# Row terms of the decay matrices as the bias of ScalarE's exponentials, in a two-block fp32 network on one core

## The reference, cut to what matters

```python
a_cs = jnp.cumsum(dtc * a, axis=2)
seg = a_cs[:, :, :, None] - a_cs[:, :, None, :]
lower = jnp.tril(jnp.ones((L, L), dtype=bool))[None, None, :, :, None, None]
decay = jnp.exp(jnp.where(lower, seg, -jnp.inf))
y_diag = jnp.einsum('bclsg,bclsgr,bcsgrp->bclgrp', cb, decay, xd)
```

```python
d_log = jnp.where(causal, b[..., :, None] - b[..., None, :] + ig[..., None, :], -jnp.inf)
m_t = jnp.maximum(inter_log, jnp.max(d_log, axis=-1))
scores = jnp.einsum('bhctd,bhcsd->bhcts', q, k) * jnp.exp(d_log - m_t[..., None])
```

## Time and profile before

| what | value |
|---|---|
| median of 3 runs | 1845.61 us (1844.77 to 1845.63) |
| the profiled execution's own time | 1845.08 us |
| its span | 1843.3 us |
| PE busy | 1828.3 us (99%) |
| DVE busy | 1266.7 us (69%) |
| ACT busy | 1055.9 us (57%) |
| POOL busy | 100.5 us (5%) |
| chain that ended last, by engine | PE 95%, ACT 3%, DVE 1% |

### The profile page before, as it was taken

One profiled execution on the slowest core, in us unless ns is written; L12 is line 12 of the kernel. 1 busy time (PEld: TensorE's weight loads), 2 busy tenths in 40 slices (PEclk: granted clock), 3 DMA queues, 4 the chain that ended last, 5 costly groups with the idle time before them and its releaser, 6 DMA issues.

```text
span 1843.3 us, 28625 instructions
## 1 busy us (share of the span) xinstructions
PE 1828.3 (99%) x11626; PEld 1628.1 (88%) x11626; DVE 1266.7 (69%) x1944; ACT 1055.9 (57%) x1557; POOL 100.5 (5%) x85
## 2 busy tenths in 40 slices
PE   9999999999999999999999999999999999999999
PEld 9998998789998999899789998988878888887887
DVE  6764797766665665588876665687667567875755
ACT  6444767565444444576755544475776456568642
POOL 0000110000000000020000000002001000210100
PEclk9999999999999999999999999999999999999999
DMA  8555542345555556553325555554445555534553
GB/s 292 193 191 182 188 151 100 106 137 189 192 193 186 190 195 194 180 179 112 126 92 172 191 193 189 173 184 147 139 137 182 194 163 182 171 126 137 172 192 116
DMA packets 86596, 310.09 MB, mean 168 GB/s; under 512 B 9648, under 2 KB 10288, under 8 KB 86464
## 3 DMA queue, kind: packets, MB, share of 16 engines
q1 hardware_dynamic: 85680, 306.35, 50.7%
q0 software_dynamic: 496, 1.65, 0.2%
q10 hardware_dynamic: 288, 0.25, 0.0%
HBM read 307.16 MB, written 1.05 MB: 167 GB/s over the span
## 4 chain that ended last, share of the span: by engine, by line
PE 95%; ACT 3%; DVE 1%; issue 0%; DMA 0%; POOL 0%; SPq 0%; DVEq 0%; ACTq 0%
PE bank L1162 92%; PE bank L1159 3%; ACT PA L1579 1%; DVE PA L2686 0%; ACT MP L1579 0%; ACT WH L1579 0%; ACT L1579 0%; DVE WL L2034 0%; DMA X<-in_x_dram 0%; ACT ET L1579 0%; DVE PC L2711 0%; DVE STATS L2384 0%; ACT BZ L1579 0%; DVE BO L2676 0%; DVE X L2120 0%
## 5 line engine op out<-in xcount | busy, mean ns | idle before, releaser
L2034 DVE TENSOR_TENSOR WL<-RAW,WH 128x1024 fp32r<-128x1024 f32 x585 | 704.6, 1213 | 405.0 <-ACT WH L1579 403.4
L1579 ACT ACTIVATE WH<-RAW 128x1024 fp32r<-128x1024 f32 (+2 forms) x587 | 610.1, 1050 | 497.0 <-PE bank L1162 494.2
L1162 PE MATMUL bank<-WH,FR 128*128 128x512 f32 x1264 | 318.4, 390 | 0.0
L1162 PEld LDWEIGHTS bank<-WH,FR 128*128 128x128 f32 x1264 | 233.7, 188 | 48.4 <-issue 0.8
L1162 PE MATMUL bank<-XTH,WH 128*128 128x256 f32 x1792 | 254.4, 279 | 0.6 <-ACT XTH L1579 0.6
L1162 PE MATMUL bank<-XTH,WL 128*128 128x256 f32 x1792 | 251.9, 278 | 0.0
L1162 PE MATMUL bank<-XTL,WH 128*128 128x256 f32 x1792 | 251.1, 277 | 0.0
L1162 PEld LDWEIGHTS bank<-XTH,WH 128*128 128x128 f32 x1792 | 226.9, 188 | 1.5 <-issue 0.8
L1162 PEld LDWEIGHTS bank<-XTH,WL 128*128 128x128 f32 x1792 | 226.7, 188 | 0.0
L1162 PEld LDWEIGHTS bank<-XTL,WH 128*128 128x128 f32 x1792 | 226.0, 188 | 0.0
L1162 PE MATMUL bank<-WL,FR 128*128 128x512 f32 x632 | 173.7, 389 | 0.0
(11 more groups left out here) (337 smaller groups left out, 1850.6 us busy)
## 6 DMA issues: line engine op xcount, KB each, us to landing
RAW<-in_WALL_dram SPq DMA_DIRECT2D x569, 512.0 KB, 3.3
RAW<-in_WALL_dram SPq DMA_DIRECT2D x8, 448.0 KB, 3.3
RAW<-in_WALL_dram SPq DMA_DIRECT2D x8, 256.0 KB, 2.6
X<-in_x_dram SPq DMA_DIRECT2D x4, 256.0 KB, 5.5
out_dram<-X SPq DMA_DIRECT2D x4, 256.0 KB, 2.0
ROWP<-in_ROWP_dram POOLq DMA_DIRECT2D x1, 672.0 KB, 11.0
CONSTS<-in_CST_dram POOLq DMA_DIRECT2D x1, 664.0 KB, 7.9
ROUNDED<-in_CSTR_dram POOLq DMA_DIRECT2D x1, 208.0 KB, 12.2
```

The costliest lines, as they stand in the source:

```text
L1162: return self.e.matmul(out, lhs, rhs, start=start, stop=stop, skip_group_check=True)
L1579: return self.e.activation(out, in_, func, **k)
L2034: self.e.tensor_tensor(lo, raw, hi.bitcast(F32), ALU.subtract).then_inc(*self.up("lo", j))
```

## The change

The row terms leave PE and become the bias operand of ACT's exponential. A bias is one number per partition, so a bank needs one instruction for each head and direction: four of 128 columns in place of one of 512 in `seg`, two (256 and 128 columns) in place of one of 384 in `mse`. The bias tiles are `BI` (in `SPT`), made from the logarithms of the step sizes less the cumulated sums that `ex` leaves in its bank, by a new DVE phase `ex`; and `BIH` (in `SP2`), copied by ACT from two more transposes in `chain` 7. The tile `LN` and its POOL memset go, `cum` loses its four products with `LN`, `DA` is made by four DVE instructions in place of eight, and the low part of `LBH` and of `LB` is made for 32 partitions in place of 64.

```diff
@@ PE.cum, PE.seg, PE.chain, PE.mse
-                self.mm(o, k.DA[:, t, d, :], (k.LE, k.GE)[d], t == 0 and d == 0, False)
-                m = self.mm(o, k.LN[:, t, d, :], k.EYE, False, True)
+                m = self.mm(ps[:, 256 * t + 128 * d:256 * t + 128 * d + 128], k.DA[:, t, d, :], (k.LE, k.GE)[d],
+                            t == 0 and d == 0, True)
...
-            self.mm(ps[:, :, x, :], k.TO[:, h0 + x:h0 + x + 1].to_broadcast([128, 128]),
-                    k.LBH[:, 256 * t:256 * t + 256].rearrange("p (d s) -> p d s", d=2), False, False)
-        for d in range(2):
-            m = self.mm(ps[:, d, :, :], k.LBH[:, 256 * t + 128 * d:256 * t + 128 * d + 128],
-                        k.FROM[:, h0:h0 + 2].unsqueeze(2).to_broadcast([128, 2, 128]), False, d == 1)
+            m = self.mm(ps[:, :, x, :], k.TO[:, h0 + x:h0 + x + 1].to_broadcast([128, 128]),
+                        k.LBH[:, 256 * t:256 * t + 256].rearrange("p (d s) -> p d s", d=2), False, x == 1)
...
+            for t in range(2):
+                m = self.tr(ps[:, 128 + 128 * t:256 + 128 * t], k.G2[:, 3, 128 * t:128 * t + 128])
...
-        self.mm(ps[:, 0:256], k.LB[:, 0:128], frm.to_broadcast([128, 256]), False, False)
-        self.mm(ps[:, 256:384], k.LB[:, 128:256], frm.to_broadcast([128, 128]), False, True).then_inc(*self.up("mse_pe", (i, h)))
@@ Scalar.seg, Scalar.mse
-        self.act(k.ET[:, n % 4, :], k.PS[k.bank["seg", i, n]][:, :], ACT.Exp).then_inc(*self.up("et_act", (i, n)))
+        g, t, q = n // 8, n // 4 % 2, n % 4
+        w.wait_ge(*self.at("ex_dve", i))
+        for d in range(2):
+            for x in range(2):
+                at, h = 256 * d + 128 * x, 8 * g + 2 * q + x
+                m = self.act(k.ET[:, n % 4, at:at + 128], k.PS[k.bank["seg", i, n]][:, at:at + 128], ACT.Exp,
+                             bias=k.BI[:, t, d, h:h + 1])
+        m.then_inc(*self.up("et_act", (i, n)))
...
-        self.act(k.E2[:, h % 3, :], k.PS[k.bank["mse", i, h]][:, 0:384], ACT.Exp).then_inc(*self.up("ms_act", (i, h)))
+        w.wait_ge(*self.at("em_act", i))
+        for t, c0, c1 in ((0, 0, 256), (1, 256, 384)):
+            m = self.act(k.E2[:, h % 3, c0:c1], k.PS[k.bank["mse", i, h]][:, c0:c1], ACT.Exp, bias=k.BIH[:, t, h:h + 1])
+        m.then_inc(*self.up("ms_act", (i, h)))
@@ Vector.ex
+        w.wait_ge(*self.at("ex_act", i))
+        w.wait_ge(*self.at("decay_act", (i, "ln")))
+        e.tensor_tensor(k.BI, k.BI, ps, ALU.subtract).then_inc(*self.up("ex_dve", i))
@@ WORK
-    "cum": "P198 A60 V140", "ex": "P281 A27",
+    "cum": "P90 A60 V70", "ex": "P170 A27 V20",
-    "seg": "P53 A61 V90",
+    "seg": "P56 A124 V90",
-    "mse": "P68 A40 V71",
+    "mse": "P42 A65 V71",
```

More of the change, by code:

```diff
@@ L757, in pair @@
             if p == 0:
-                for phase in (("chain", i, 6), ("hconv_silu", i, 0), ("hconv_silu", i, 1), ("evict", ("bv", i, 0))):
+                for phase in (("chain", i, 7), ("hconv_silu", i, 0), ("hconv_silu", i, 1), ("evict", ("bv", i, 0))):
                     yield phase
@@ L1742, in decay @@
             w.wait_ge(*self.at("decay_dve", (i, "ln")))
-            self.act(k.LN[:, :, :, 64:80], k.LN[:, :, :, 64:80], ACT.Ln)
-            self.act(k.LN[:, :, :, 96:112], k.LN[:, :, :, 96:112], ACT.Ln).then_inc(*self.up("decay_act", (i, "ln")))
+            self.act(k.BI, k.BI, ACT.Ln).then_inc(*self.up("decay_act", (i, "ln")))
     def lat_sq(self, i, t):
@@ L1900, in chain @@
             w.wait_ge(*self.at("chain_pe", (i, 7)))
-            self.act(k.EM[:, :, :], k.PS[k.bank["chain", i, 7]][:, 0:128].rearrange("p (t h) -> p t h", t=2)[:, :, 0:8],
-                     ACT.Exp, scale=-1.0).then_inc(*self.up("em_act", i))
+            ps = k.PS[k.bank["chain", i, 7]]
+            self.act(k.BIH, ps[:, 128:384].rearrange("p (t h) -> p t h", t=2)[:, :, 64:72], ACT.Copy)
+            self.act(k.EM[:, :, :], ps[:, 0:128].rearrange("p (t h) -> p t h", t=2)[:, :, 0:8], ACT.Exp, scale=-1.0).then_inc(
+                *self.up("em_act", i))
     def lam(self, i, x):
@@ L1995, in program @@
             "qk_sum": self.qk_sum, "qk_norm": self.qk_norm, "rope1": self.rope1, "qk_rope": self.qk_rope, "sc": self.sc,
-            "mo_a": self.mo_a, "mo_var": self.mo_var, "mo_y": self.mo_y, "cum": self.cum,
+            "mo_a": self.mo_a, "mo_var": self.mo_var, "mo_y": self.mo_y, "cum": self.cum, "ex": self.ex,
             "state_x": self.state_x, "fin": self.fin, "seg": self.seg, "skip": self.skip, "mid": self.mid, "fin_y": self.fin_y,
@@ L2277, in decay @@
             w.wait_ge(*self.at("pads_pool", i))
-            for at in (64, 96):
-                m = e.tensor_scalar(k.LN[:, :, :, at:at + 16], k.DT[:, :, :].rearrange("p t (d h) -> p t d h", d=2), 1e-18, None, ALU.max)
-            m.then_inc(*self.up("decay_dve", (i, "ln")))
+            e.tensor_scalar(k.BI, k.DT[:, :, :].rearrange("p t (d h) -> p t d h", d=2), 1e-18, None, ALU.max).then_inc(
+                *self.up("decay_dve", (i, "ln")))
             for d in range(2):
                 a = k.SPT[:, 5, 16 * d:16 * d + 16].unsqueeze(1).to_broadcast([128, 2, 16])
-                e.tensor_tensor(k.DA[:, :, d, 64:80], k.DT[:, :, 16 * d:16 * d + 16], a, ALU.mult).then_inc(*self.up("decay_dve"))
-            w.wait_ge(*self.now("decay_dve"))
-            for d in range(2):
-                for at, sgn in ((96, 1.0), (0, -1.0), (32, -1.0)):
-                    m = e.tensor_scalar(k.DA[:, :, d, at:at + 16], k.DA[:, :, d, 64:80], sgn, None, ALU.mult)
+                for at in (0, 32):
+                    m = e.scalar_tensor_tensor(k.DA[:, :, d, at:at + 16], k.DT[:, :, 16 * d:16 * d + 16], -1.0, a, ALU.mult, ALU.mult)
             m.then_inc(*self.up("decay_dve", (i, 3)))
@@ L2418, in cum, with ex @@
         w.wait_ge(*self.at("cum_act", i))
-        e.tensor_tensor(k.LBH[32:64, :], ps[32:64, :], k.LBH[32:64, :].bitcast(F32), ALU.subtract)
-        e.tensor_tensor(k.LBH[96:128, :], ps[96:128, :], k.LBH[96:128, :].bitcast(F32), ALU.subtract).then_inc(*self.up("cum_dve", i))
+        e.tensor_tensor(k.LBH[32:64, :], ps[32:64, :], k.LBH[32:64, :].bitcast(F32), ALU.subtract).then_inc(*self.up("cum_dve", i))
+    def ex(self, i):
+        k, w, e = self.k, self.w, self.e
+        ps = k.PS[k.bank["ex", i]][:, 0:128].rearrange("p (t d x) -> p t d x", t=2, d=2)[:, :, :, 0:16]
+        w.wait_ge(*self.at("ex_act", i))
+        w.wait_ge(*self.at("decay_act", (i, "ln")))
+        e.tensor_tensor(k.BI, k.BI, ps, ALU.subtract).then_inc(*self.up("ex_dve", i))
     def state_x(self, i, d):
@@ L2795, in mix_pads @@
         e.memset(k.PR[:, :, 257:258], 0.0)
-        e.memset(k.LN[:, :, :, :], 0.0)
         e.memset(k.DA[:, :, :, :], 0.0).then_inc(*self.up("pads_pool", i))
```

18 lines of the change are left out of this document (8 added, 10 removed), and 8 rows, old and new, of the table WORK.

## The result

| | before | changed |
|---|---|---|
| median | 1845.44 us (1844.77 to 1845.63, 4 runs) | 1855.76 us (1853.03 to 1858.18, 4 runs) |
| ratio to before | | 1.0056, 95% interval 1.0044 to 1.0069 |
| the profiled execution's own time | 1845.08 us | 1858.18 us |
| its span | 1843.3 us | 1856.3 us |
| mean granted TensorE clock | 1.000 | 0.996 |

The account below looks back on a forecast made before the run. PE, busy 99% of the span, was taken to bound the kernel. From 1845.1 us, mixers add 4.0, hybrid layers take off 1.4, and 0.5 is added for the median: 1848.2 us, range 1837 to 1857.

Parts of the forecast that it names:

- Products removed: On PE in mixers, hybrid layers and cum: 7.0 + 3.5 + 1.8 us removed, 0.9 added for transposes, net 11.4 us less.
- ACT's prices: On ACT: a four-piece segment bank takes 1.16 us, 0.57 more; the bias operand 0.09; an mLSTM bank grows by 0.25.
- Rival 2: In both segment stretches ACT becomes the bound, over 0.2% slower from 1.23 us a bank: 1853 to 1860 us, chance 0.22.
- The walk up to the flips: First mixer's segments, walked: waits of 0.2 to 2.1 us at cn_a, cn_b and several applies; stretch ends at 43.0.
- The 6.4 us of new waits: In a mixer's segment stretch: 2.9 us longer though PE's products are 3.5 us less, so 6.4 us of new waits.
- The mixer's term: Each mixer: segments 2.9 us longer, less 0.9 in cum, so 2.0 us more; 4.0 for two.
- Hybrid layers: Both hybrid layers together: 2.6 us kept from the products less 1.2 lost in the attention, 1.4 us faster.
- The mLSTM part: mLSTM banks of the hybrid layers: ACT's longer exponentials stay hidden behind a weight block, so 3.5 - 0.9 = 2.6 us are kept.
- the new order in the attention: Differential attention: head 3's exponentials stand behind the eviction of BO, between two table loads; 0.6 us a layer, 1.2 in all.
- the split behind head 3: Hybrid layers' attention: PE waits 1.9 us for a split (WH) behind head 3; some 1.3 us of waiting go in exchange.
- Rival 3: Shifted order changes waits of attention heads or the hybrid layers' last stretch by 3 to 5 us either way; chance 0.08.
- The full price of the removed products: On PE: all of the net 11.4 us less work counts on the path as long as PE has no new wait.

Follow-up runs that it names:

- seg_only: Kernel before with only the mixers' part of the change (seg, cum, ex, BI), in the old phase order: 1852.05 us, ratio 1.0029.
- mse_only: Kernel before with only the hybrid layers' part of the change (mse, chain 7, BIH, LB), in the old phase order: 1842.20 us, ratio 0.9981.
- fill: Changed kernel plus ten products of 512 columns on PE in each mixer, ahead of the block that waits for FR: 1852.63 us, ratio 1.0033.
- order_new: Kernel before, code unchanged, with the changed numbers in WORK and so the changed kernel's phase order: 1856.28 us, ratio 1.0058.
- no_from: Kernel before without the two row-term products of each segment bank, ACT and order unchanged: 1842.23 us, ratio 0.9983.
- pieces_bias: Kernel before with each segment exponential as four of 128 columns with a bias operand, all products kept, old order: 1855.78 us, ratio 1.0052.
- after_again: The changed kernel run and profiled again, unchanged: 1856.77 us, ratio 1.0059 to the kernel before.
- fix_ys: Changed kernel with the last fin_y of each mixer moved behind the two flips of the scaled rows: 1854.71 us, ratio 1.0050.
- code_old: Changed code with the old numbers in WORK for seg, mse, cum, ex and chain7, so the old phase order: 1848.64 us, ratio 1.0014.

## Why the prediction was right in range and wrong in size

- **Products removed: right.** `cum` gained 0.9 us a mixer (in `seg_only` the distance falls from 0.04 at `RBC,CONSTS` to -0.86 at `DA,CONSTS` behind it), eight mLSTM banks gained 1.8 us in `mse_only`. PE's records fell by 108: by the 112 of the prediction, and rose by 4, not 8, since a transpose is one record. The four transposes cost 0.4 us together, not 0.9.
- **ACT's prices: right.** A bank of four was put at 1.16 us and takes 1.14; the operand at 0.09 and takes 0.375 - 0.289 = 0.086; an mLSTM bank was to grow by 0.25 and takes 0.73 where it took 0.49. Rival 2's condition, a bank of 1.23 us or more, was not met. The estimate of 1.27 us from the Trainium skill ("ScalarE: Activation LUTs", "What ACT_TABLE_LOAD costs") was 0.13 too high, its 93 ns for the operand fits.
- **The walk up to the flips: right to the place, too high in most sizes.** In the first mixer it gave `cn_a` 0.55 more (0.76 was measured: 1.05 less the 0.29 of the earlier trace rows), `apply` 0 0.4 (0.25), the second `cn_b` 0.9 (0.61), the two later ones 1.1 and 0.25 (0.17 in all), `apply` 8 2.1 (1.42), `apply` 10 1.35 (1.11), and 0.2, 0.25 and 0.5 at `apply` 1, `apply` 3 and the flips (nothing). The rows in brackets are idle time; by the starts of the products `apply` 8 comes 1.58 us late and `apply` 10 1.27. It had the stretch end at 43.0 us; from the first `seg` at 344.80 to the end of the flips at 386.87 it is 42.1, but the block behind them starts at 389.40, after 44.6.
- **The 6.4 us of new waits: right in size by luck.** The walk's own list adds up to 7.6 us; the 6.4 of the sum are the difference of the two ends. Measured are 4.3 us of new idle time up to the flips, and 2.5 us behind them, for `FR`, which the walk didn't have.
- **The step that failed: the walk stopped at the flips.** "The two flips behind the last `apply` wait 0.5 for the scaled rows. The changed stretch ends at 43.0." They don't wait; but the block behind them needs `FR`, and on ACT the `YT` of the last `fin_y` stands ahead of it. With the rows of before it could have been walked: `YT` waits for two `XS` on DVE, which come after `apply` 15 and a split in DVE's list, and PE's 2.53 us for `FR` behind it are the largest single wait of the changed kernel. The walk looked for places where an exponential is late and stopped behind the last one; ACT is late beyond it.
- **A rival that was missing: the clock.** The sum took every wait at its own length. Behind these waits PE ran at 1.2 GHz for a while, 1.7 us of lost full-speed time in the first mixer of the profiled run and some 5 in the second (part of it while PE was idle anyway), and `fill` points to PE's idleness as what does it. The Trainium skill, "TensorE: Matmul & The Clock Gate", section "HAM oscillation — how this bites in real kernels", tells of a kernel in which PE waits for a DMA after each short piece of its work and starts the next piece at the slow clock. The waits there are longer than any here, so it was a warning against this change and no price for it; the traces agree with it in kind, by the 3.56 us of the block behind the 2.53 us of waiting. The earlier trace rows shows 1.00 for the kernel before, whose waits in that stretch are 0.3 us at most, which made the term easy to leave out.
- **The mixer's term** was thus 2.0 us and was 4.3 to 4.6 in most cases, up to 7.0 with two drops. With the clock up (`fill`, second mixer) it is 2.7.
- **The range held the time by luck.** Its upper part was there for a bank that costs ACT more than the 1.16 us taken. The bank costs 1.14, and what filled that part are the wait for `FR` and the clock.
- **Hybrid layers: sign right, terms smaller and larger.** The mLSTM part gave 3.3 us, not 2.6, and the new order in the attention took 2.3, not 1.2; the sum was -0.9 where -1.4 was predicted. The wait for the split behind head 3 is there as told (1.28 us, predicted 1.9).
- **Rival 3** is small and of the other sign: from `cum` to the first `seg` the new order gains some 0.7 us (`order_new` is 2.0 us further behind at the first `seg` than at `RBC,CONSTS`, with a block more, which is 2.7).
- **The full price of the removed products** ("all of it on the path as long as PE has no new wait") was not reached even in the old order. That they are worth 3.3 to 3.6 of 7.0 us when ACT gets nothing more (`no_from`) shows how near the old stretch already was to its other engines; the earlier trace rows, 59% busy for ACT, doesn't show it.

What remains open: why the second mixer's drop at 933 us comes in one execution and not in the next, why `order_new` has no drop behind its second wait for `FR`, and what share of the 3.4 us or so that `no_from` misses is clock and what is waits: the 0.83 over 10 us of its second mixer is 1.7 us.

## What to carry to other kernels

Work moved from a full engine to a half idle one is free only if its new latency fits between the neighbours in the in-order list of that engine: here 0.8 us a bank was nearly free, 1.15 us cost more than the products were worth. Walk a changed order up to the first block that again needs nothing of the stretch, and count every instruction ahead of each result on its engine. Changed costs in a planner's table are a change of their own; time them apart from the code, since a good part (here the mLSTM half) may be hidden under a bad order.

## What the runs showed of the hardware

- A per-partition bias operand costs an ACTIVATE of 128 columns 0.086 us (0.375 against 0.289 us), 0.36 us over the four of a bank.
- Behind four waits of 2.5 us (`FR`, two profiles of the changed kernel) the granted TensorE clock fell, to 0.50 to 0.70 in the lowest window of 3 us; of two waits of 2.27 us (`order_new`) one was followed by a drop. Several waits of 0.3 to 0.8 us close together were followed by drops too, to 0.66 (`seg_only`) and 0.50 (`pieces_bias`). With products issued into the wait (`fill`) it stayed at 1.00 both times.
- At the start of the program, three warm-up products (six records) took 2.77 us in one execution and 1.46 in another while the granted clock of the windows stood at 1.00 in both: there the rows' durations show what the clock column doesn't. Waits for `X` of 0.71, 0.80 and 1.20 us were followed by slow products (`after_again`, the changed kernel, `mse_only`), waits of 0.71, 1.05, 1.08 and 1.10 us were not (`fix_ys`, `pieces_bias`, `seg_only`, `code_old`).
- A transpose of fp32 data stands in the trace as one record, a product of plain fp32 operands as two.
